# A hybrid decoder block on one core: the first two weight pairs by operand, and four column groups for the heads' near levels and the meta tokens

## The reference

```python
h = rms_norm(z, norm_w)                      # z is meta tokens, then x
q, fz, iv, g_hg, u, g_pool, m_hg, m_pool = split(h @ w_in + b_in)   # eight matrices of 1024 columns
f = lb + (1 - lb) * sigmoid(fz);  k = (1 - lb) * sigmoid(-fz)
S_t = diag(f_t) S_{t-1} + k_t v_t^T;  o_t = S_t^T q_t               # 8 heads of 128 x 128
y_hg = (rms_norm(o) * silu(g_hg)) @ w_down_hg
y_pool = (mix(window means of u) * silu(g_pool)) @ w_down_pool      # windows 2, 4, 8, 16
z = z + (sigmoid(m_hg) * y_hg + sigmoid(m_pool) * y_pool) @ w_out
out = rms_norm(z, final_norm_w)[16:]
```

## Time and profile before

| | |
|---|---|
| three runs | 1139.19, 1140.01, 1140.18 us, median 1140.01 |
| profiled execution | 1139.84 us, its span 1138.1 us |
| TensorE matmul busy | 1095.0 us, 96% of the span |
| VectorE, ScalarE, GpSimd busy | 815.9, 478.3, 92.7 us |
| mean granted clock of TensorE | 0.988 of full speed |

### The profile page before, as it was taken

How to read it: one execution, slowest core, us unless ns; L and a number is a source line. 1 busy time by engine, 2 the same in 40 slices (tenths; PEclk the granted TensorE clock), 3 DMA queues, 4 the chain that set the end, 5 groups by cost and what they waited for, 6 DMA issues and landing times. The chain is left out here.

```text
span 1138.1 us, 16080 instructions
## 1 busy us (share of the span) xinstructions
PE 1095.0 (96%) x6044; PEld 903.9 (79%) x6044; DVE 815.9 (72%) x1343; ACT 478.3 (42%) x807; POOL 92.7 (8%) x154
## 2 busy tenths in 40 slices
PE   7798999999999999999999999999999999999996
PEld 6577888888888888888788878778887787787884
DVE  7856787787868686878757577685557879989233
ACT  6552443425252535243334343344445536336122
POOL 2300000000000000101010000001100011000111
PEclk8998999999999999999999999999999999999998
DMA  6011102011111111102121212213722384555233
GB/s 226 20 57 54 38 19 67 27 56 38 56 37 57 38 57 37 57 21 78 60 93 38 84 56 87 88 48 137 270 89 97 113 330 150 197 191 175 93 97 116
DMA packets 35900, 103.91 MB, mean 91 GB/s; under 512 B 4560, under 2 KB 4560, under 8 KB 35824
## 3 DMA queue, kind: packets, MB, share of 16 engines
q1 hardware_dynamic: 21920, 65.09, 17.8%
q0 software_dynamic: 8240, 26.79, 6.3%
q10 hardware_dynamic: 5664, 11.02, 2.7%
HBM read 77.71 MB, written 25.17 MB: 90 GB/s over the span
## 5 line engine op out<-in xcount | busy, mean ns | idle before, releaser
L1088 PE MATMUL acc<-r_hi,w_hi 128*128 128x512 f32 x1120 | 453.2, 405 | 12.6 <-DVE r_lo L1965 4.3
L1088 PE MATMUL acc<-r_hi,w_lo 128*128 128x512 f32 x1120 | 439.2, 392 | 0.0
L1088 PE MATMUL acc<-r_lo,w_hi 128*128 128x512 f32 x1120 | 438.1, 391 | 0.0
L1088 PEld LDWEIGHTS acc<-r_hi,w_hi 128*128 128x128 f32 x1120 | 211.0, 188 | 60.5 <-issue 8.1
L1088 PEld LDWEIGHTS acc<-r_hi,w_lo 128*128 128x128 f32 x1120 | 210.9, 188 | 46.2
L1088 PEld LDWEIGHTS acc<-r_lo,w_hi 128*128 128x128 f32 x1120 | 211.4, 189 | 39.3
L637 ACT ACTIVATE w_hi<-sum 128x512 fp32r<-128x512 f32 x160 | 100.0, 627 | 167.7 <-PE acc L1088 84.5
L1451 DVE TENSOR_TENSOR w_lo<-sum,w_hi 128x512 fp32r<-128x512 f32 x160 | 109.3, 687 | 66.6 <-ACT w_hi L637 66.3
L1451 DVE TENSOR_TENSOR w_lo<-raw,w_hi 128x512 fp32r<-128x512 f32 x120 | 82.1, 687 | 67.2 <-ACT w_hi L637 67.1
L637 ACT ACTIVATE w_hi<-raw 128x512 fp32r<-128x512 f32 x120 | 74.7, 624 | 26.8 <-PE acc L1088 26.8
L715 ACT ACTIVATE second<-acc,bias 128x512 f32<-128x512 f32 x32 | 21.9, 684 | 77.4 <-PE acc L1088 77.3
(11 more groups left out here) (270 smaller groups left out, 1530.9 us busy)
## 6 DMA issues: line engine op xcount, KB each, us to landing
raw<-in_wstream SPq DMA_DIRECT2D x88, 512.0 KB, 3.6
xin<-in_x SPq DMA_DIRECT2D x8, 512.0 KB, 4.1
a_spill<-gt POOLq DMA_DIRECT2D x16, 256.0 KB, 3.4
c_spill<-pg POOLq DMA_DIRECT2D x16, 256.0 KB, 2.7
stage<-a_spill ACTq DMA_DIRECT2D x4, 1024.0 KB, 12.7
smh_spill<-zq POOLq DMA_DIRECT2D x16, 256.0 KB, 2.5
gate_in<-smh_spill SPq DMA_DIRECT2D x16, 256.0 KB, 5.1
part_spill<-zq POOLq DMA_DIRECT2D x16, 256.0 KB, 5.0
```

Source lines behind the costliest of these rows:

```text
L1088: ins = pe.matmul(out_ap, a, b, start=first and n == 0, stop=final and n == 2, skip_group_check=partial)
```

## The change

**The first two pairs by operand.** `EARLY = 2` and a new `ORDER`: (0,0) (0,1) (1,0) (1,1), then product 5 of both pairs, 3 of both, 2, 4 and 6 of both. Pair 1 gets its own places for sums (`sums_early`), for its second raw block (`raw_early`, one more transfer), for product 5's bank (`lev`), and its `second` and `fifth` (in `prod` and `gs`). B12 and B22 of tiles 5 to 8 are copied whole to SBUF, so that the banks come free after ScalarE's three copies; V5, V6, V7 and V4 are made from these copies, in halves, and V5 is needed fourth. Five token buffers take the place of three. `h_transposes(5)` moves behind product (0,0), and tile 6 into the middle of product (0,1). The squares run a tile ahead of the copies on ScalarE; the four sums of pair 0 leave the stretch ahead of the first product. `prepare_copies(0)` moves ahead of `last_quarter(0)`.

**Near levels.** Steps 0 to 3 work on the 32 x 32 blocks at the diagonal only: four matmuls a chunk, 32 columns of keys each against 32, 32, 48 or 16 queries, at output partitions 0, 32, 64 and 96. VectorE's `copy_predicated` writes `att_near` (256 columns for all chunks), one instruction where there were two or four, and ScalarE's new `spread_near` copies it to `att` in four instructions a head. Level 0 waits for the spread of the head before, `outputs` for its own.

**Meta tokens.** `hm` holds them unsplit. `meta_product` runs in products 0 and 3 only and multiplies them with the raw float32 weights, contraction block k at output partitions 32k. `mt` and the stack have 128 rows. The loads of raw blocks now also wait for `meta_mm`.

```diff
-ORDER = [(0, 0), (0, 1), (1, 0), (1, 1)] + [(p, i) for p in range(2) for i in range(2, 6)] + [(0, 6), (1, 6)]
+EARLY = 2
+ORDER = [(0, 0), (0, 1), (1, 0), (1, 1)] + [(p, i) for i in (5, 3, 2, 4, 6) for p in range(EARLY)]
...
+GROUP = 32
+GROUPS = P // GROUP
+NEAR = {0: 32, 1: 32, 2: 48, 4: 16}
...
                     if p < N_PAIRS:
-                        sp.wait_ge(S["sums_made"], 4 * p + 4)
+                        sp.wait_ge(S["sums_made"], 4 * max(p + 1, EARLY))
                         sp.wait_ge(S["w_lo"], POS[p, 6 if n else 1] + 1)
+                        if p in META_AT:
+                            sp.wait_ge(S["meta_mm"], META_AT[p] + n + 1)
...
+            def spread_near(r):
+
+                act.wait_ge(S["level_done"], r * STEPS + 4)
+                after(act, S["o_mm"], r)
+                by_chunk = att[:, :].rearrange("p (c t) -> p c t", c=CHUNKS)
+                for g in range(GROUPS):
+                    rows = slice(g * GROUP, (g + 1) * GROUP)
+                    ins = act.activation(by_chunk[rows, :, rows], att_near[rows, :, :], ACT.Copy)
+                ins.then_inc(S["near_spread"], 1)
...
-                slot, c = POS[p, i] % RING, {0: 0, 1: 1, 3: 0, 6: 2}[i]
-                for k in range(KH):
-                    w = slice(k * P, (k + 1) * P)
-                    for m, part in enumerate((w_hi, w_lo)):
-                        ins = pe.matmul(acc[3 - n][0:2 * META, 0:P], hm[:, c, k, :], part[slot][:, w],
...
+                for h in range(2):
+                    for k in range(KH):
+                        ins = pe.matmul(acc[3 - n][k * GROUP:(k + 1) * GROUP, 0:P], hm[:, h, k, :],
+                                        raw_half(p, n, h)[:, k * P:(k + 1) * P], start=h == 0, stop=h == 1)
+                ins.then_inc(S["meta_mm"], 1)
...
-                if m == 2:
-                    pe.wait_ge(S["v_copied"], r + 1)
...
+                    if m <= 4:
+                        for g in range(GROUPS):
...
+                            n = NEAR[m]
+                            ins = pe.matmul(lev[g * GROUP:(g + 1) * GROUP, c * n:(c + 1) * n],
+                                            kt[:, META + t.start:META + t.stop], q, start=True, stop=True)
                         continue
...
-            keep_warm(4)
-            h_transposes(5)
             keep_warm(6)
             product(0, 0)
+            h_transposes(5)
+            half(0, 1, 0)
             h_transposes(6)
-            product(0, 1)
+            half(0, 1, 1)
             h_transposes(7)
             product(1, 0)
             h_transposes(8)
...
+            early_fifth(0)
+            low(8)
+            low(9)
+            v7_sum(0)
+            v7_sum(1)
+            early_third_sum(0)
+            early_third_sum(1)
```

More of the change, by code:

```diff
@@ L47 @@
 SUM_MADE = {S1: 1, S3: 2, S2: 3, S4: 4}
+EARLY_SUMS = [(p, s) for p in range(2) for s in (S1, S2, S4)] + [(0, S3), (1, S3)]
 RING = 4
@@ L318, in hybrid_block @@
         part_dram = nc.dram_tensor("part_spill", [NK, 2, P, HALF], F32, kind="Internal").ap()
-        x_loaded = (S["x_loaded0"], S["x_loaded1"], S["x_loaded2"])
+        x_loaded = tuple(S[f"x_loaded{n}"] for n in range(5))
         raw_loaded = (S["raw_loaded0"], S["raw_loaded1"], S["raw_loaded2"])
@@ L957, in _ @@
                     during(q, i)
+                    if i == 3:
+                        spread_near(r)
                 copy_k(r)
@@ L1146, in half @@
                         after(pe, S["c21_done"], p - 1)
-                        for n in range(2):
-                            if p > 1 and p - 1 - n in META_AT:
-                                pe.wait_ge(S["meta_placed"], META_AT[p - 1 - n] + n + 1)
+                        if p > 1 and p - 1 in META_AT:
+                            pe.wait_ge(S["meta_placed"], META_AT[p - 1] + 1)
                     elif i == 1:
@@ L1301, in _ @@
             h_transposes(8)
-            product(1, 1)
-            for p, i in ORDER[4:2 * PRODUCTS]:
+            for p, i in ORDER[3:2 * PRODUCTS]:
                 product(p, i)
@@ L1566, in entries @@
+                if m == 4:
+                    steps.mark(dve.copy_predicated(att_near[:, :, 16:32],
+                                                   mask[:, MASKS - 1:MASKS, 0:16].to_broadcast([P, CHUNKS, 16]), near(4)))
                     return
                 a, p = level_view(att[:, :], m, 1), lev[:, :].rearrange("p (b j) -> p b j", j=1 << m)
-                if m < LEVELS - 2:
-                    a, p = (v.rearrange("p (c b) j -> p c b j", c=CHUNKS) for v in (a, p))
-                    steps.mark(dve.copy_predicated(a, mask_of(MASKS - 1, 1 << m, CHUNKS), p))
-                    return
@@ L1708, in _ @@
             x_mean(2)
+            dve.wait_ge(S["logits_loaded"], 16)
+            steps.mark(dve.tensor_tensor(lmax[:, :], logits[:, 0, :], logits[:, 1, :], ALU.max))
+            steps.settle()
+            for n in range(2):
+                ins = dve.tensor_tensor(lexp[:, n, :], logits[:, n, :], lmax[:, :], ALU.subtract)
+            ins.then_inc(S["lb_shifted"], 1)
             h_row(2)
-            dve.wait_ge(S["hm_copied"], 1)
-            dve.tensor_tensor(hmf[:, 2], hmf[:, 1], hmf[:, 0], ALU.subtract).then_inc(S["hm_made"], 1)
-            weight_sums(0, (0,))
             x_mean(3)
@@ L1792, in _ @@
             dve.tensor_scalar(one_minus_lb[:, :], lb[:, :], -1.0, 1.0, ALU.mult, ALU.add).then_inc(S["lb_made"], 1)
+            v6_sum(0)
+            v6_sum(1)
+            low(7)
+            v6_low(0)
+            v6_low(1)
+            early_fifth(0)
[5 more added lines that the diff above has]
+            early_third_sum(1)
+            v7_low(0)
+            v7_low(1)
+            low(10)
+            v4_sum(0)
+            v4_sum(1)
+            add_12(0)
+            low(11)
+            add_22(0)
+            v4_low(0)
+            v4_low(1)
+            low(12)
+            early_fifth(1)
             add_12(1)
+            low(13)
+            add_22(1)
+            dve.wait_ge(S["masks_spread"], 1)
+            prepare(0)
             low(14)
```

506 lines of the change are left out of this document (264 added, 242 removed).

## The result

The changed kernel takes 1082.01 us (1081.81 to 1082.87 in 4 runs) against 1140.0 before (1139.19 to 1140.18): a ratio of 0.9494, 95% interval 0.9478 to 0.9511, or 58 us less. Forecast were 1084.0 and 56 us less.

What follows compares the result with a forecast made beforehand. The prediction took TensorE as the bound, busy 1095.0 of 1138.1 us. Near levels 29.7, meta products 7.7, meta turns 6.2 and the start 12 sum to 55.6 us off 1139.84, forecast 1084 us, range 1074 to 1115.

Steps and rivals of the forecast that it cites:

- Near levels: Steps 0 to 3 of each head on four column groups: 3.71 us saved a head, 29.7 us for eight.
- a quarter of the lone price: Near-step records: four groups run at once, so each costs a quarter of 32 ns (32 columns) or 45 ns (48).
- only neighbours overlap: Rival: never more than two groups at once, near steps 1.33 us (step 2 1.75), total 1113 us; chance 0.17.
- the floor of issue: Rival: TensorE cannot start records faster than 16 ns apart, near steps cost as on two groups, 1102 us; chance 0.10.
- The slower rival: Four column groups in turn run one at a time, near steps 2.36 us (step 2 3.2), 1171 us; chance 0.04.
- Meta products: Two new calls of 0.76 us a pair for four of 0.54: 0.64 saved a pair, 7.7 us for twelve.
- Meta turns: 24 turns fall from 0.51 to 0.25 us, no longer differing in shape from their neighbours: 6.2 us saved.
- The start: Up to step 0 of head 0: earlier first product, fewer long stalls and less half clock save 12 us, bounds 4 and 18.
- eight stalls walked out ahead: Waits of TensorE in the new start, 0.7 to 2.1 us each, together 11 in place of 12.4 us.
- The 6 us put down for it: In the start, half clock after stalls costs half of what was busy in it, 6 us, and should mostly not come.
- What hides beside it: Work of VectorE and ScalarE beside TensorE, `spread_near`, raw-load waits and the added transfer: costed at nothing.
- The overhead of 60 cycles for each matmul: Skill's rule, spoken against: 64 records would take an estimated 1.6 us, and a near step would gain nothing.

Runs made afterwards that it cites:

- run 4: The changed kernel with the 32 matmuls of a near step issued group by group instead of chunk by chunk over the four groups: 1122.69 us in one execution.
- Run 2: The kernel before with only the meta tokens changed (unsplit, four column groups, two products and two turns a pair): 1126.58 us, ratio 0.9887.
- run 3: The kernel before with near levels and meta tokens both changed and the start as before: 1094.23 us, ratio 0.9602.
- run 10: The kernel of run 3 with 36 identity matmuls in the wait ahead of step 0 of head 0: 2.1 us more than run 3.
- 11: The kernel of run 10 with 17 identity matmuls in place of 36: 1093.24 us, ratio 0.9598.
- run 6: The changed kernel with the second meta product of seven head pairs moved beside step 0, into the bank small: 1079.41 us against 1081.16 for the changed kernel.

## Why the prediction was right

- **Near levels, 29.7 forecast.** 30.6 measured alone (28.8 to 32.1 by the interval), 28.8 by the starts of the steps. The choice of a quarter of the lone price was right, by two errors that cancel: the lone price is 27 and 36 ns, not 32 and 45 (run 4), and four groups give not 4 but 3.1 to 3.4. The rival "only neighbours overlap" (16 ns a record, 1.33 us a step) fell with step 1 of the changed kernel, and the floor of issue as well: 9 ns is below its 16. The slower rival describes run 4: groups that come one after the other cost 2.05 us a step 1, and the time is 41 us more.
- **Meta products, 7.7 forecast.** By the starts a call alone costs 0.78 where 0.76 was forecast, and a pair gains 0.57, 6.8 in all. In the whole change it is 2.4 us more, since the first product stands beside step 0 and shares its fixed part. The prediction priced 0.31 us for each call, wherever it stands; that is the step that was mis-sized, in the safe direction.
- **Meta turns, 6.2 forecast.** 0.23 us each in place of 0.52, 24 of them: 7.0. The size is right and the reason only half: the 0.09 on entry is gone, the cost on leaving isn't (0.08 is left of 0.11). The old step 1, with its 128 columns, paid it too, so it is no price of a change of shape. The two records take 0.15 where 0.25 was forecast, which makes up for it. Run 2 confirms products and turns together: 13.2.
- **The start, 12 forecast.** 12.2 by runs 3 and the changed kernel. The first product was forecast near 23 us and runs at 23.44, step 0 of head 0 near 79 and starts at 80.75. Of the eight stalls walked out ahead (11 us) seven are in the trace, each within 0.8 us of its size: (0,5) 1.44 for 0.7, (1,3) 1.59 for 1.6, (0,2) 0.42 for 1.0, (0,4) 1.25 for 1.9, (1,4) 1.65 for 1.9, (0,6) 1.51 for 2.1, pair 2 0.92 for 1.2. (0,3) doesn't wait, (1,5) does, 0.60; together 9.4. The half clock does not come in the changed kernel's trace, as forecast. The 6 us put down for it were partly wrong. The term took what TensorE loses in a slow stretch for what the program loses. What TensorE loses was read rightly; here is the longest stretch in the kernel before:

```profile
91.26 3.78 PE L1224 MATMUL levels<-ek,kt 128*128 128x128 f32 x16 [4.44 <-ACT qx L845]
...
97.03 0.40 PE L1088 MATMUL acc<-r_hi,w_hi 128*128 128x512 f32 x1
```

That is 5.77 us for work that takes 3.00 at full clock three heads later (274.00 to 277.00), 2.8 lost as forecast; in run 3, with its narrow records, 2.3 (runs 10 and 11). But the first of the three stretches runs into the next wait, and with the clock back there nothing was won (run 10, 1.5 us). For the second no run shows which it is. The sum also left out a cost: the transposes of tile 5 (0.88 us of TensorE) stand behind the first product now. So the total of the start is closer to its forecast than its terms are, which is in part luck.
- **What hides beside it.** Costed at nothing, and in the heads it is nothing: a head is 55.1 us where 55.4 was forecast, VectorE fell by 4.8 in it, `spread_near` delays nobody, and no wait of TensorE in a head but the 0.3 us for the states is left to pay. In the pooling it is about 1 us: the meta products of the U pairs wait 2.1 us for VectorE's `pg` in two places, where it was 1.1 before.
- **The overhead of 60 cycles for each matmul**, by which a near step would gain nothing, isn't there in this form: 64 records take 0.76 us. So the trace disagrees with the Trainium skill, TensorEngine Tiling (Array Packing), section Instruction Overhead, but by less than the prediction made of it. The prediction charged the 60 cycles to each record. Charged to each of the 32 matmuls of a step they give an estimated 0.8 us, or 25 ns a matmul, where the trace has about 18: a near step gains either way.

## What to carry to other kernels

Where small matmuls have free columns, put neighbours in program order on different column groups: the order alone decided between 0.76 and 1.92 us for the same 64 records. Then set such calls side by side, since each isolated burst pays about a third of a microsecond to get in and out. And read a stall twice: once as idle time, once as the clock behind it (2.3 us behind the wait of 4.4, by two traces). Then ask what stands behind the slow stretch: if it is another wait, for work that another engine ends no sooner, the half clock costs nothing (run 10). Short stalls are safer but not safe: in the changed kernel's trace none of them, 1.9 us the longest, is followed by half clock, but in four other traces of kernels with the same wait of 1.91 us it is, for 1.5 us.

## What was not expected of the hardware

- Bursts in 32-column form that touch share their fixed cost of 0.34 us, over a change of the weights' source, of the moving shape and of the bank (1.33 us for 0.89 + 0.78; 1.57 to the next large matmul with a third burst). A 32-column burst beside one of 128 columns shares nothing (2.56 for 1.79 + 0.78).
- The interval behind a burst is too long whether the burst has another shape (0.11 us behind step 1) or the shape of its neighbours (0.08 behind a new meta turn). The 0.09 us ahead of it is another matter: the near steps and the new meta products pay it, the new turn doesn't. The old meta product, which also used 32 columns, didn't pay it either (300.71 - 300.48 = 0.23), so the change of shape alone doesn't explain it; no run tested what does.
- The same wait of 1.91 us ahead of the same work is followed by half clock in four traces and not in four others (run 6).
- Where step 0 and the meta product touch, their records are interleaved by start: the first record of the product starts at 245.74 us, one of step 0 at 245.75. The Trainium skill, TensorE: Matmul & The Clock Gate, Part 3, has matmuls in the order of the program in start and end; these starts, 10 to 20 ns apart, differ from it.
- POOL and VectorE held each other up on operations with two SBUF inputs: 2.29 us became 3.38 and 0.68 became 1.18, and a sum on POOL 1.63 or 3.22.
